# Level products of a chunked linear attention: 64 instead of 128 moving columns, taken through strided views

## What is computed

```python
def chunk_gla(q, k, v, logf, s0):
    # S_t = diag(exp(logf_t)) S_{t-1} + k_t v_t^T, o_t = S_t^T q_t, evaluated in chunks
    ...
    def step(S, inp):
        qi, ki, vi, gi = inp
        b = jnp.cumsum(gi, axis=1)
        dec = jnp.exp(jnp.where(causal, b[:, :, None] - b[:, None, :], -jnp.inf))
        a = jnp.einsum('bthk,bshk,btshk->bhts', qi, ki, dec)
        o = jnp.einsum('bthk,bhkv->bthv', qi * jnp.exp(b), S) + jnp.einsum('bhts,bshv->bthv', a, vi)
        bl = b[:, -1]
        S = jnp.exp(bl)[..., None] * S + jnp.einsum('bshk,bshv->bhkv', ki * jnp.exp(bl[:, None] - b), vi)
        return S, o
```

## Time and profile before

| what | us |
|---|---|
| median of 3 runs | 4149.31 (4149.23 to 4151.43) |
| the profiled execution, its own time | 4146.77 |
| its span, first to last instruction | 4145.0 |
| TensorE busy in the span | 3528.2 |
| VectorE, ScalarE, GpSimd busy | 1356.5, 1346.7, 1491.0 |
| L1130, 896 instructions, busy | 123.8 |
| mean granted TensorE clock | 0.906 of full |

### The profile page before, as it was taken

One profiled execution on the slowest core, in us unless ns is written; L12 is line 12 of the kernel. 1 busy time (PEld: TensorE's weight loads), 2 busy tenths in 40 slices (PEclk: granted clock), 3 DMA queues, 4 the chain that ended last, 5 costly groups with the idle time before them and its releaser, 6 DMA issues. The chain is left out here.

```text
span 4145.0 us, 63868 instructions
## 1 busy us (share of the span) xinstructions
PE 3528.2 (85%) x22287; PEld 3308.2 (80%) x22287; DVE 1356.5 (33%) x2012; ACT 1346.7 (32%) x2200; POOL 1491.0 (36%) x964
## 2 busy tenths in 40 slices
PE   5988885897088887799999996888887799999997
PEld 5966664897067777699999996877777699999997
DVE  3034441001003445443343333043244443333341
ACT  2144441000003443234343442223223234343442
POOL 2300001342302222246666663122122236666664
PEclk9888886898569989899999998898999799999998
DMA  1400001784200001124444443110101124444443
GB/s 69 137 5 0 0 0 47 256 264 150 76 16 26 31 31 57 57 92 140 133 137 148 144 149 97 42 32 30 42 32 57 68 81 142 132 142 135 139 139 125
DMA packets 158152, 372.98 MB, mean 90 GB/s; under 512 B 22410, under 2 KB 78026, under 8 KB 156316
## 3 DMA queue, kind: packets, MB, share of 16 engines
q1 hardware_dynamic: 116828, 310.96, 23.0%
q10 hardware_dynamic: 29440, 32.78, 2.4%
q0 software_dynamic: 11776, 27.80, 2.0%
HBM read 352.76 MB, written 22.89 MB: 91 GB/s over the span
## 5 line engine op out<-in xcount | busy, mean ns | idle before, releaser
L493 POOL TENSOR_TENSOR back_WL<-back_RAW,back_WH 128x1024 fp32r<-128x1024 f32 (+1 forms) x408 | 955.8, 2349 | 682.6 <-ACT back_WH L594 681.0
L532 PE MATMUL PS<-back_TH,back_WH 128*128 128x344 f32 x2112 | 677.3, 321 | 14.6 <-DVE back_TL L703 14.6
L532 PE MATMUL PS<-back_TL,back_WH 128*128 128x344 f32 x2112 | 675.4, 320 | 0.0
L532 PE MATMUL PS<-back_TH,back_WL 128*128 128x344 f32 x2112 | 675.1, 320 | 0.0
L594 ACT ACTIVATE back_WH<-back_RAW 128x1024 fp32r<-128x1024 f32 (+1 forms) x408 | 421.6, 1033 | 525.1 <-DMA back_RAW<-in_w 354.0
L532 PEld LDWEIGHTS PS<-back_TH,back_WH 128*128 128x128 f32 x2112 | 398.4, 189 | 16.3 <-issue 12.1
L532 PEld LDWEIGHTS PS<-back_TL,back_WH 128*128 128x128 f32 x2112 | 398.4, 189 | 0.0
L532 PEld LDWEIGHTS PS<-back_TH,back_WL 128*128 128x128 f32 x2112 | 398.3, 189 | 0.0
L741 DVE TENSOR_TENSOR back_HL<-back_TMP,back_HH 128x344 f32 x132 | 322.4, 2443 | 129.0 <-ACT back_HH L607 129.0
L1066 PE MATMUL PS<-layer_XH,layer_WH 128*128 128x344 f32 x960 | 328.0, 342 | 29.9 <-POOL layer_WL L1016 28.2
L532 PE MATMUL PS<-back_HH,back_WH 128*128 128x344 f32 x1056 | 338.4, 320 | 0.0
(11 more groups left out here) (358 smaller groups left out, 6129.6 us busy)
## 6 DMA issues: line engine op xcount, KB each, us to landing
back_RAW<-in_w SPq DMA_DIRECT2D x360, 512.0 KB, 3.3
layer_AR<-in_cmp SPq DMA_DIRECT2D x192, 128.0 KB, 4.2
layer_AR<-in_cmp POOLq DMA_DIRECT2D x192, 128.0 KB, 4.1
back_RAW<-in_w SPq DMA_DIRECT2D x48, 384.0 KB, 3.1
layer_AR<-in_cmp ACTq DMA_DIRECT2D x128, 128.0 KB, 4.0
layer_WR<-in_w_even SPq DMA_DIRECT2D x54, 256.0 KB, 2.8
layer_WR<-in_w_odd SPq DMA_DIRECT2D x50, 256.0 KB, 2.9
XT<-in_xT SPq DMA_DIRECT2D x4, 1032.0 KB, 7.8
```

The lines of the kernel that those rows point to most:

```text
L493: pool.tensor_tensor(lo, raw, hi.bitcast(F32), ALU.subtract).then_inc(wl_ready, 1)
L532: mm = pe.matmul(m.PS[:, bank, 0:CH], wgt[:, t % RING, w], tok[:, k0 + k], start=(k0 + k + n == 0), stop=(last and n == 2 and k == kt - 1))
```

## The change

In every chunk of a head but the first, each level product takes only the 64 query columns of second halves, as the moving side, and writes only the 64 columns of `b_y` at the same places. Both views have blocks of h = 64 / 2^lv columns, every second block: one block of 64 at level 0, pairs of 2 at level 5, every second column at level 6. The number and the order of instructions, the stationary tiles and all waits stay. In the first chunk of a head all 128 columns are computed, so that the columns left out later hold that chunk's products, which L1427 goes on multiplying by zero. The mask, the sum and everything else are unchanged.

```diff
                 for lv in range(LEVELS):
-                    pe.matmul(b_y[:, lv * P:(lv + 1) * P], KS[:, c % 2, lv], QS[:, c % 2, 1 + lv],
-                              start=True, stop=True)
+                    n, out, q = 1 << lv, b_y[:, lv * P:(lv + 1) * P], QS[:, c % 2, 1 + lv]
+                    if c > 0:
+                        out = out.rearrange("p (b c h) -> p b c h", b=n, c=2)[:, :, 1]
+                        q = q.rearrange("p (b c h) -> p b c h", b=n, c=2)[:, :, 1]
+                    pe.matmul(out, KS[:, c % 2, lv], q, start=True, stop=True)
                 pe.matmul(b_y[:, LEVELS * P:], kT[:, c * P:(c + 1) * P], qT[:, c * P:(c + 1) * P],
                           start=True, stop=True).then_inc(a_ready, 1)
```

## The result

| | before | changed |
|---|---|---|
| median of 4 runs, us | 4150.37 (4149.23 to 4152.98) | 4178.17 (4174.99 to 4183.15) |
| ratio, with 95% interval | | 1.0069 (1.0057 to 1.0081) |
| profiled execution, its own time, us | 4146.77 | 4183.15 |
| its span, us | 4145.0 | 4181.6 |

The change made the kernel 27.8 us slower, 0.7%; forecast were 4171 us within 4154 to 4194. The profiled execution of the changed kernel was the slowest of its four, so its span shows more, 36.6 us.

What follows compares the result with a forecast made beforehand. Bound by TensorE, busy 85% of the span, with VectorE waiting for its level-product bursts. 4146.8 us profiled + 0 + 22 + 0 + 0 = 4168.8 us; with 2.5 us for the median, 4171 us (+0.5%), range 4154 to 4194 us.

Steps and rivals of the forecast that it cites:

- Spacing 0: Level-product bursts in later chunks: weight loads set the pace, so 64 moving columns take as long as 128; change 0 us.
- The clock, +22 us: Two last heads: TensorE's granted clock falls after thin bursts and returns after the sums; about +22 us, between 0 and 45.
- The price of a whole half-clock chunk, 3.22 us: Last heads: a chunk wholly at half clock pays +1.70 us for burst with diagonal and +1.52 for sums and outputs.
- The picture of burst and sums taking turns: Last heads: in each chunk either the burst or the sums and outputs run slow, 21 to 24 us over 14 chunks.
- Filled heads, 0: Six filled heads: projections behind each chunk's outputs keep the clock at 1.00, so the change costs 0 us.
- the cover: Filled heads: the 344-column projections behind each chunk's outputs, taken to keep TensorE's clock at 1.00.
- The 10 us given as its bound: Filled heads: if the clock goes in one place of each head, 6 x 1.7 = 10 us; in the range, not the sum.
- Strided views, 0: Strided burst outputs, level 6 every second column: 0 us, as twice the time per column still fits the slot.
- Faster, 0.07: Rival, chance 0.07: moving columns set the burst spacing, 0.06 to 0.08 us; -37 us in all, 4112 us.
- No change, 0.10: Rival, chance 0.10: last heads have enough work beside the burst, the clock holds at 1.00; 4149 us.
- What VectorE would wait for: If the clock is lost, VectorE, whose L1427 waits only 0.28 us for the diagonal in a last head, waits for each burst.

## Why the prediction was right, and where a term was off

- **Spacing 0**: right. The loads of a changed burst at full clock take 1.68 us as before, and with a stationary side of 64 the pace halves. L1694, 16 columns under a 128-column stationary side, was the right row to go by. The Trainium skill ("TensorE: Matmul & The Clock Gate", Back-to-back issue gap) says that in a stream of weight loads and products both set the spacing, and that its formula by moving columns alone is for a single product by itself. This trace agrees: with half the moving columns the loads kept their pace, (1.68 - 0.19) / 13 = 0.115 us in this burst before and after.
- **The clock, +22 us**: right in place and mechanism, and near in size. The two last heads took 26.8 us more in the profile, the slowest execution of the four, and the run with the change there alone lost 0.55%, 23 us. The price of a whole half-clock chunk, 3.22 us, was exact: 6.86 + 3.22 = 10.08, measured 10.09. How many chunks would pay it was the guess: 14.4 / 3.22 is 4.5 of 7 in HGRN. The picture of burst and sums taking turns was only half right; HGRN's head alternated at first and then stayed at half for its last four bursts of 3.78 us. The sum also stopped at the last chunk, and the products behind it cost 3.4 us more. One row was read too far: the stretch from 620 to 645 us at 1.00 holds products of up to 512 moving columns (L1665) beside those of 128, and L1578 and L2278 have a stationary side of 64. So the earlier trace rows alone do not single out the moving columns; the runs with the change in the last heads alone and without a stride do.
- **Filled heads, 0**: too low. This is the term that was mis-sized. The run with the change there alone lost 0.14% (0.02 to 0.25), some 6 us, in HGRN's heads, where the cover has a hole at and beside the fifth chunk; GLA's filled heads kept theirs. The prediction had that hole in the earlier trace rows, but judged the cover by 20 us of the earlier trace rows that end where it begins (1320 us). The 10 us given as its bound hold. The 23 and 6 us of the two runs stand against 22 and 0 in the sum, and together they are about the 27.8 us measured.
- **Strided views, 0**: right. Without the stride the loss stays, and with 64 on both sides the strided level 6 keeps a pace of 0.058 us. "Advanced Engine Details and Errata" (PSUM Cachelines) of the Trainium skill says that non-contiguous PSUM patterns slow products much. At one f32 column in two this case's trace does not agree: where such a slowdown would have shown, at 0.058 us, there was none.
- **Faster, 0.07**: its deciding figure, a spacing of 0.06 to 0.08 us in the bursts, was not seen; 0.058 us came only with a shorter stationary side. **No change, 0.10**: the last heads did not hold 1.00.
- What VectorE would wait for was foreseen: 91.5 us behind the diagonal in place of 79.0, though its own work was the same.

## What to carry to other kernels

Before cutting the moving columns of a product, see whether they set its pace: find a product of the trace with the same stationary side and fewer columns, and compare the spacing of the two. Where they do not, the cut saves nothing and makes TensorE's stretch thinner, and in a stage that is mostly waits this may cost the clock for everything else in the chain. In such a stage idle products in waits that exist anyway are worth a run: here they took back the change's loss, and ahead of the first chunks they made the kernel before 0.23% faster (with those in the last heads as well 0.25%, no difference between the two).

## What was not expected of the hardware

- The clock did not follow the columns left out in proportion. With 3 of 7 levels halved the last heads kept 47.3 and 50.6 us, with 7 they took 61.7 and 63.1. What decides between the two is not shown.
- Longer busy is not a firmer clock: in the changed last head TensorE is busy 46.5 of 61.7 us at 0.61, before 31.1 of 47.3 at 0.96. The busy share rises as the clock falls, and tells nothing of why.
- Idle products of 512 columns between dependent steps cost no measurable time: 5 a chunk in 16 chunks left the last heads of the kernel with 128 columns at 47.4 and 50.7 us, as before (47.3 and 50.7).
